# A decoder step on one core: u and Q in three passes, x's low halves kept in memory, the sample's ties ahead of the pooled products

## The reference

```python
h = rms_norm(x, ln1);  z = h @ w_in               # u | q | k | v | idx q | idx key | idx weights | gates
a_pool = pool_mixer(u, ...)                       # 4 groups of 128 channels, trailing windows 2, 4, 8, 16:
                                                  # (window mean - token) @ pool_w[g], * pool_scale
idx = indexer_select(qi, wi, ki, ...)             # top min(256, L/4) causal keys of each row
a_attn = attend(q, k[idx], v[idx], ...)           # softmax(q k * HD**-0.5 + bias) v; samples read paged caches
g = sigmoid(gates)
m = g[..., :D] * (a_pool @ w_pool_proj) + g[..., D:] * (a_attn @ w_attn_proj)
h = x + m @ w_out
y = rms_norm(h + (silu(f1) * f2) @ w_down)        # f1, f2 = rms_norm(h, ln2) @ w_gate_up
```

## Time and profile before

| | us |
|---|---|
| runs: median (lowest to highest) | 1597.32 (1594.06 to 1599.57) |
| the profiled execution's own time | 1594.21 |
| its span | 1591.7 |
| PE busy in the span | 1535.0 (96%) |
| DVE busy | 925.1 (58%) |
| POOL busy | 607.7 (38%) |
| ACT busy | 573.4 (36%) |

### The profile page before, as it was taken

How to read it: one execution, slowest core, us unless ns; L and a number is a source line. 1 busy time by engine, 2 the same in 40 slices (tenths; PEclk the granted TensorE clock), 3 DMA queues, 4 the chain that set the end, 5 groups by cost and what they waited for, 6 DMA issues and landing times.

```text
span 1591.7 us, 25832 instructions
## 1 busy us (share of the span) xinstructions
PE 1535.0 (96%) x9489; PEld 1377.6 (87%) x9489; DVE 925.1 (58%) x2173; ACT 573.4 (36%) x1171; POOL 607.7 (38%) x548
## 2 busy tenths in 40 slices
PE   7998999989999999999999999999999999999997
PEld 5873566657996677999999999999999999999997
DVE  5427987787964775222448755455555454555546
ACT  4324364324314665222335422413224223132233
POOL 4111019274654321111123834626437255273450
PEclk9999999997998999999999999999999999999999
DMA  5431011132110011321012201102102011021002
...
DMA packets 91555, 87.58 MB, mean 55 GB/s; under 512 B 17046, under 2 KB 82214, under 8 KB 91469
## 3 DMA queue, kind: packets, MB, share of 16 engines
...
## 4 chain that ended last, share of the span: by engine, by line
PE 58%; DVE 1%; POOL 1%; issue 1%; ACT 0%; POOLq 0%; DVEq 0%
PE banks L2031 27%; PE banks L2128 16%; PE banks L108 13%; DVE yo L2605 0%; PE banks L1988 0%; PE banks L1969 0%; PE banks L2145 0%; POOL wL L2179 0%; ACT XH L2247 0%; POOL hnL_lo L2192 0%; DVE hnL_hi L2460 0%; POOL dL L2176 0%; POOL T4L L2192 0%; ACT sH L2240 0%; ACT resid L2244 0%
## 5 line engine op out<-in xcount | busy, mean ns | idle before, releaser
L2179 POOL TENSOR_TENSOR wL<-w_raw,wH 128x512 fp32r<-128x512 f32 x176 | 231.1, 1329 | 315.1 <-ACT wH L2290 313.9
L2031 PE MATMUL banks<-hnH,wH 128*128 128x344 f32 x704 | 225.9, 321 | 2.1 <-POOL wL L2179 0.8
L2031 PE MATMUL banks<-hnH,wL 128*128 128x344 f32 x704 | 224.7, 319 | 0.0
L2592 DVE TENSOR_TENSOR resid<-resid,banks 128x344 f32<-128x344 f32 x264 | 131.9, 511 | 96.9 <-PE banks L2128 96.9
L2128 PE MATMUL banks<-aH,dH 128*128 128x344 f32 x528 | 169.2, 321 | 0.0
L2128 PE MATMUL banks<-aH,dL 128*128 128x344 f32 x528 | 169.1, 320 | 0.0
L2128 PE MATMUL banks<-aL,dH 128*128 128x344 f32 x528 | 168.2, 319 | 0.0
L1483 DVE TENSOR_SCALAR_CACHE_REDUCE pta<-SC,thr 128x384 uint8<-128x384 f32 (+4 forms) x160 | 144.0, 930 | 2.2 <-POOL SC L921 0.2
L2290 ACT ACTIVATE wH<-w_raw 128x512 fp32r<-128x512 f32 x176 | 109.6, 626 | 73.3 <-PE banks L2031 40.5
L2031 PEld LDWEIGHTS banks<-hnH,wH 128*128 128x128 f32 x704 | 132.2, 188 | 3.2 <-issue 1.8
L2031 PEld LDWEIGHTS banks<-hnH,wL 128*128 128x128 f32 x704 | 132.2, 188 | 0.0
...
## 6 DMA issues: line engine op xcount, KB each, us to landing
w_raw<-in_w_gate_up_dram SPq DMA_DIRECT2D x22, 1024.0 KB, 5.0
d_raw<-in_w_down_dram SPq DMA_DIRECT2D x11, 1024.0 KB, 4.8
big<-in_w_in_dram SPq DMA_DIRECT2D x12, 512.0 KB, 3.6
W<-in_x_prompt_dram SPq DMA_DIRECT2D x8, 512.0 KB, 5.7
slab_raw<-in_w_in_dram SPq DMA_DIRECT2D x8, 512.0 KB, 3.8
x_nat<-in_x_prompt_dram SPq DMA_DIRECT2D x8, 512.0 KB, 4.2
slab_raw<-in_w_out_dram SPq DMA_DIRECT2D x8, 512.0 KB, 3.6
out_dram<-yo SPq DMA_DIRECT2D x8, 512.0 KB, 2.6
```

The lines of the kernel that those rows point to most:

```text
L2031: last = mm(out, W_[w][s][:, i * P:(i + 1) * P], x_of(x)(i), start=start and i == 0 and j == 0, stop=stop and i == HALF - 1 and j == 2)
L2179: gp.tensor_tensor(wL[s].rearrange("p (k n) -> p k n", k=HALF), quadrant(x, *HOME[name]), f32(wH[s]).rearrange("p (k n) -> p k n", k=HALF) ...
L2592: V.tensor_tensor(resid[:, m, chunk(DOWN_ORDER[o])], resid[:, m, chunk(DOWN_ORDER[o])], ps[:, 4 + n % 4, 0:CH], ALU.add).then_inc(y_done, 1)
```

## The change

1. Normalised x goes to a ring of two tiles, `xT`. ACT writes its high part straight into `XH`; DVE's low part is stored by SP to a DRAM tensor `x_lows` tile by tile. It is loaded again twice: as `ZL` ahead of u and Q, and as `XL` ahead of the gates, k 4 to 7 after the last sample logits, k 0 to 3 after the last projected chunk. `high_x`, `keep_x` and `low_x` are gone.
2. u and Q are made in three passes. Their eight slabs are split by `high_uq` on ACT (slabs 0 and 1 in the score stage, 2 to 7 behind the copies of chunks 2, 5, 7, 10, 14 and 17) and by `low_uq` on POOL (0 and 1 in the loop that hides later keys, 2 behind it, 3 to 5 ahead of the mixer, 6 and 7 behind its first and second group). SP loads slab n when slab n-2 is split.
3. The sample's scores are joined after chunk 0 and transposed after chunk 1. `EARLY_ROUNDS` is 18. The single early rounds among ties, lanes and ranks are gone, two instead of three stand ahead of the own list, all the rest behind the near keys. ACT issues up to 25x/16 of its rounds by chunk x, instead of 7x/4 - 1.
4. The ties are summed ahead of the pooled products, before PE waits for `pooled`; lanes are summed behind the second group of the products, ranks turned behind the last. `list_keys` stands ahead of projected chunk 4 (the fifth), `begin_sample_logits` ahead of 7.
5. On ACT `high_slab(0)`, `values_out` and `high_slab(1)` follow one another; on POOL `low_slab(0)` and `low_slab(1)` follow the value gathers. PE's first gate chunk waits for the loads of `XL`.

The diff, cut to its core:

```diff
+    x_lows = nc.dram_tensor("x_lows", [P, KD, TOK], F32).ap()
...
+            ZL = place("ZL", 0, [KD, TOK], F32R, Z_at)
+            XZ_ = {"hi": XH, "lo": ZL}
...
-            EARLY_ROUNDS = 23
+            EARLY_ROUNDS = 18
...
+                def store_low(t):
+                    sp.wait_ge(split_lo, t + 1)
+                    sp.dma_start(x_lows[:, :, tile_cols(t)], f32(xnL[:, t % 2, :, 0:rows(t)])).then_inc(x_lo_out[t % 2], 16)
...
                 for n in range(U_ITEMS):
                     if n >= 2:
-                        sp.wait_ge(uq_ready, 3 * (n - 1))
+                        sp.wait_ge(slab_lo, POOL_PIECES + n - 1)
                     load_slab(n % 2, slice(C_U + n * P, C_U + (n + 1) * P))
+                    if n == 1:
+                        for b in range(2):
+                            sp.dma_start(f32(ZL[:, 4 * b:4 * b + 4, :]), x_lows[:, 4 * b:4 * b + 4, :]).then_inc(x_lo_in[b], 16)
...
+                sp.wait_ge(sm_made, SM["S_ready"])
+                sp.dma_start(f32(XL[:, 4:8, :]), x_lows[:, 4:8, :]).then_inc(x_lo_in[0], 16)
+                sp.wait_ge(p_ready, PROJ)
+                sp.dma_start(f32(XL[:, 0:4, :]), x_lows[:, 0:4, :]).then_inc(x_lo_in[1], 16)
                 sp.wait_ge(sm_made, SM["probs_turned"])
...
                 def slab_chunk(x):
                     n, c = divmod(x, NCH)
                     if c == 0:
-                        pe.wait_ge(big_in[n % 2], 16 * (n // 2 + 1) if n < U_ITEMS else 32 + 32 * ((n - U_ITEMS) // 2 + 1))
+                        pe.wait_ge(slab_lo, POOL_PIECES + n + 1)
                     if x >= ROT:
                         pe.wait_ge(uq_evac, x - ROT + 1)
+                    slab = uq_slab(n)
                     for k in range(KD):
-                        last = mm(ps[:, x % ROT, 0:CH], big[:, n % 2, k, :], hT[:, k, chunk(c)], start=k == 0, stop=k == KD - 1)
+                        if x == 0 and k % 4 == 0:
+                            pe.wait_ge(x_lo_in[k // 4], 16)
+                        for j, (w, v) in enumerate((("hi", "hi"), ("hi", "lo"), ("lo", "hi"))):
...
                     slab_chunk(x)
+                    if x == 0:
+                        join_sample_heads()
                     if x == 1:
-                        join_sample_heads()
-                    if x == 2:
                         transpose_sample_scores()
...
+                sum_sample_ties()
                 pe.wait_ge(poolw_in, 16)
                 pe.wait_ge(pooled, NG)
...
-                before = {0: [sum_lanes], 1: [turn_ranks], 5: [list_keys], 8: [begin_sample_logits],
+                before = {4: [list_keys], 7: [begin_sample_logits],
...
-                            if m == 0:
-                                pe.wait_ge(xh_done, units.index((c, k)) + 1)
+                            if x == 0 and a % 4 == 0:
+                                pe.wait_ge(x_lo_in[a // 4], 32)
...
+                def low_uq(n):
+                    pool.wait_ge(slab_hi, PIECES + n + 1)
+                    if n % 4 >= 2:
+                        pool.wait_ge(uq_ready, 3 * (n - 1))
+                    slab = uq_slab(n)
+                    gp.tensor_tensor(slab["lo"][:, :], raw[:, n % 2, :], f32(slab["hi"][:, :]), ALU.subtract).then_inc(slab_lo, 1)
...
+                    if g < 2:
+                        low_uq(6 + g)
...
+                def high_uq(n):
+                    act.wait_ge(big_in[n % 2], 16 * (n // 2 + 1) if n < U_ITEMS else 32 + 32 * ((n - U_ITEMS) // 2 + 1))
+                    if n % 4 >= 2:
+                        act.wait_ge(uq_ready, 3 * (n - 1))
+                    A(uq_slab(n)["hi"][:, :], raw[:, n % 2, :], ACT.Copy).then_inc(slab_hi, 1)
...
+                HIGH_AT = {2: 2, 5: 3, 7: 4, 10: 5, 14: 6, 17: 7}
+
                 def rounds_before(x):
-                    return min(32, max(0, (7 * x) // 4 - 1))
+                    return min(32, (25 * x) // 16)
...
-                    A(xnH[:, t % 2, :, 0:r], hT[:, :, tile_cols(t)], ACT.Copy).then_inc(split_hi, 1)
+                    A(XH[:, :, tile_cols(t)], xT[:, t % 2, :, 0:r], ACT.Copy).then_inc(split_hi, 1)
...
-                early_rounds(3, rej_bank)
+                early_rounds(2, rej_bank)
                 dve.wait_ge(sm_made, SM["listed"])
```

202 lines of the change are left out of this document (91 added, 111 removed).

## The result

| | us |
|---|---|
| before, median of 11 runs (lowest to highest) | 1594.90 (1594.06 to 1599.57) |
| changed, median of 11 runs | 1584.56 (1579.92 to 1591.10) |
| changed over before | 0.9930, 95% interval 0.9914 to 0.9946 |
| profiled executions | 1594.21 before, 1583.69 changed |
| their spans | 1591.7 before, 1581.9 changed |

The change gives 0.7%, 10 us, and the interval excludes both no change and the -3.3 us that I forecast. The direction of the sum was right, its size was not. 1584.56 lies at the very end of the range, and "within 0.3%", for which I gave 0.46, did not come.

What follows compares the result with a forecast made beforehand. PE (96% busy) was taken to bound the kernel, with POOL's mixer becoming the bound before the pooled products. Values 2.1 us earlier plus 1.2 in the gates gave -3.3, from 1597.3 to 1594.0 us; range 1584 to 1602.

Steps and rivals of the forecast that it cites:

- within 0.3%: Whole kernel: measured time within 0.3%, 4.8 us, of no change; chance 0.46.
- Steps 1 and 2: u/Q and mixer: PE saves 20.6 us, but POOL's mixer ends only 4.3 earlier, at 276.8, and becomes the bound.
- Step 3: Pooled products: PE's clock at half for 6 us from 276.9, costing 3.4 us.
- Step 4: Ties, lanes, ranks: ranks turned at 287.8, 7.8 us earlier; key list and key gathers 8 earlier.
- Step 5: Early rounds: DVE, with 15.5 us more behind the near keys, replaces PE's logits as the wait; L746 4.1 earlier.
- Step 6: Ahead of the probabilities: PE stands some 5 us, half clock costs 2; values stay at half clock, starting 2.1 earlier.
- rival (a): Clock holds at both new idle places: -8.7 us, 1588.6; about 1584 if values partly keep full clock; chance 0.30.
- Rival (c): Before the gates: late load of x's low halves, at half rate, makes the sum +5.6 us, 1603; chance 0.07.
- Step 7: Gates: no x splits on POOL and ACT frees gate slab 1's splits, 1.2 us; gates end 3.3 earlier.

Runs made afterwards that it cites:

- e10: Changed kernel with the two low splits among the mixer's groups left out (Q wrong in its low part there); 1582.92 us.
- e13: Changed kernel with the low halves of the last two Q slabs made on DVE instead of POOL; 1580.95 us, ratio to before 0.9916.
- e1_again: The changed kernel as it is, run again for a second profile; 1586.97 us.
- e3_pe_warm: Changed kernel with 76 products in no output run on PE while it waits for POOL's mixer; 1585.87 us.
- e7: Changed kernel with ties, lanes, ranks, key list and begin of logits back in their old places; 1591.93 us.
- e11: Kernel before with 13 products in no output among the probability transposes, keeping PE busy; 1589.00 us, ratio to before 0.9953.
- e12: Changed kernel with 13 products in no output among the probability transposes, keeping PE busy; 1585.06 us.
- e8_slab_first: Changed kernel with the second load of x's low halves cut into three pieces around the first gate slabs; 1582.83 us.
- e17: Kernel before with 10 instead of 5 rounds run ahead of the sample's softmax, so PE stops before the probabilities; 1593.89 us, ratio 1.0007.
- e18: Changed kernel with six early rounds moved into DVE's wait for the lanes, second profile; 1581.91 us in 4 runs and 1584.98 in 10 across both series.
- e4: Changed kernel with two ACT copies in no output ahead of each of the second to fourth copies of turned probabilities; 1585.77 us.
- e6: Kernel before with two pairs of ACT copies for x's splits moved from behind chunks 22 and 23 to behind the probabilities; 1596.93 us, ratio 0.9996.
- e2: Changed kernel with six early rounds moved into DVE's wait for the lanes, first profile; 1581.91 us in 4 runs and 1584.98 in 10 across both series.
- e5_before_again: The kernel before as it is, run again for a second profile; 1598.03 us.

## Why the prediction came out as it did

**Steps 1 and 2 were right.** u and Q end where they should (ties at 263.43 against 263.4). The mixer starts at 222.23 (222.1), waits 2.05 us for ACT's split of slab 6 (2.1), and ends at 276.9 (276.8). POOL became the bound and PE stood 12.90 us. e10 and e13 confirm it from the other side. The stores of x's low halves cost nothing that shows: u and Q start at 166.8 to 167.5 us in all six profiles of the two kernels, once the early half clock is taken off.

**Step 3 was right in kind and too dear.** The clock was at half at the products, for 3.1 us in the first profile and for 6 in `e1_again`. Against `e3_pe_warm`, which has full clock there, that cost 1.4 and 2.6 us at the ranks, and I had 3.4. Hence ranks at 287.8 forecast and 285.8 in the one, 290.2 - 3.1 = 287.1 in the other, whose u and Q started 3.1 later.

**Step 4 was right** (e7: 3.4 to 4.8 us at the probabilities). **Step 5 was right in that DVE takes the place of the logits,** but DVE came at 364.4 instead of 361.9. In the row at 322.19 and the two behind it DVE stood 2.25, 1.26 and 0.54 us while the keys were gathered; what it waited for is not shown. Those 4 us are more than the difference, since its own list had come 9.6 us earlier and not 8. The probabilities are 1.3 later than forecast.

**Step 6 is the one that failed.** PE stood 2.5 us ahead of the probabilities and not 5. Chunk 23 was at half clock in two of the three profiles of the changed kernel and cost 1.7 us (4.17 instead of 2.48), near the 2 that I took. The values are the error. "They ran at half clock before and I leave them so": I took the half clock of one stretch of one profile for a property of the work. It differs from execution to execution, and the changed kernel has it less often. The values took 7.8 us of PE and not 15. With the gates' wait of 1.65 the stretch from values to gates is 9.8, 5.1 us less than before (5.4 in the mean of three profiles of each). I had this case as a clause of rival (a), that the values might keep the full clock and bring the time to about 1584, for which it was the low end of the range. The rest of (a) was wrong: the clock was at half at the products in all three profiles and at chunk 23 in two. (a) reached 1584 with 5.4 us from these two places, most of which did not come, so that its number is nearly the measured one is luck. e11 shows the price of the values' clock by itself: 7 us for the kernel before. With full clock in both kernels the change is worth 2 to 4 us by e11 and e12, close to my sum.

I had also read that PE's clock was full until 334 us in the kernel before. It was not: in the same profile there is a half clock of 3.4 us from 115.5 on.

```profile
116.00:118.00 2.00, 2.00 (x11) 1.66 (x10) 0.76 (x2) 0.49 (x1) 0.00 (x0) 0.50 0.00 0
```

It was no term of my sum, though its length differs from execution to execution: "early" in the table is 0.0 to 1.7 us in the three profiles of before and 1.7 to 5.1 in those of the changed kernel.

**Rival (c) came true in part.** The gates waited for the first slab. The second load of x's low halves took 8.0 us (7.6 is the median of the two) and not the 10.6 that I had from the earlier trace rows, where the row's own sizes give 10.1. The slab took 6.9 (from its issue at 375.5 to 382.4) and not 3.6; both were under way side by side. Part 6 of the page of the changed kernel, for the earlier trace rows:

```profile
big<-in_w_in_dram SPq DMA_DIRECT2D x12, 512.0 KB, 3.8
...
XL<-x_lows SPq DMA_DIRECT2D x2, 2064.0 KB, 7.6
```

I had taken each load by itself. In `e8_slab_first`, where only a third of that load is ahead of the slab, the wait is gone. With values at full clock the slab's low half was 1.65 us late; with values at half I would not have seen it.

**Step 7 was right in its gap and too small in its sum.** From the gates' start to their last matmul are 94.6 us in the mean before and 92.1 now, and I had forecast 1.2 less. Before, the gates began with 4.7 to 5.9 us at half clock, but that cost nothing: with full clock there they take 94.6 (e11) and 94.5 (e17) too, because they wait 4.1 us for pieces of x and for the second slab. Without x's splits and without half clock they take 90.5 (e8, e12, e18). So taking the splits away is worth 4.1 us, and 1.6 of it is lost again to the 3.4 us at half clock with which the gates of the changed kernel begin. I had seen the wait at 407 and not those that the half clock covered.

The sum in the means of three profiles, counted from the first u/Q product: -2.4 at the values' start (-2.1 forecast), -5.4 between values and gates (0 forecast), -2.5 in the gates (-1.2 forecast): -10.3, as the medians differ.

**What stays open** is why the values have the full clock in 12 of 14 profiles of the changed kernel and its variants and in none of the three of the kernel before. The length of PE's thin stretch ahead of them does not sort the profiles (e4, e6), and the stop ahead of the probabilities is not needed (e2, e18); whether it helps is open (e17). The place of the fall does sort them: in the first and third profile of the changed kernel and in e17 it fell 7 to 9 us ahead of the values, at chunk 23, and was back in time; where it fell within 1.3 us of their start, it stayed down (in e7 it did both). In the other eleven it fell at neither place. What sets the place was not tested. No kernel was run that fixes what came some tens of us earlier, such as the half clock between 314 and 334 us, whose place and length differ between the kernels too. The Trainium skill (TensorE: Matmul & The Clock Gate, Part 1, "What's actually happening") has activity release the throttle. The rows at 379 to 398 and in `e5_before_again` don't agree for this stage: PE had hardly an idle moment there and stayed at 0.50 through all of the values, and the full clock came back only behind the start of the gates.
